# A hybrid decoder layer on eight cores: the mixer result added in DRAM, and other uses for the bf16 write-backs

## The reference

```
u1 = rmsnorm(x, ffn1_norm);   h = x + 0.5 * (silu(u1 @ Wg1) * (u1 @ Wu1)) @ Wd1
z = rmsnorm(h, mix_norm) @ w_in              # a_val a_gate | B C x | g_a g_b, 1024 columns each
a = causal_conv31(a_val * sigmoid(a_gate)) + bias;   a = silu(layernorm(a));   y_a = a @ a_w_out
y_b = (B * causal_conv3(C * x)) @ b_w_out
h = h + (sigmoid(g_a) * y_a + sigmoid(g_b) * y_b) @ w_o
h = h + 0.5 * (silu(u2 @ Wg2) * (u2 @ Wu2)) @ Wd2     # u2 = rmsnorm(h, ffn2_norm)
out = rmsnorm(h, final_norm)
```

## Time and profile before

| | |
|---|---|
| median of 3 runs | 3161.51 us (3161.02, 3161.51 and 3572.86) |
| the profiled execution | 3157.62 us |
| its span, slowest core (core 6) | 3156.1 us; the other cores 3136.4 to 3156.0 |
| PE / DVE / ACT / POOL busy | 96% / 78% / 28% / 6% |
| granted TensorE clock, mean | 0.988 of 2.4 GHz |
| DMA queue 1 (SP), queue 0 (POOL) | 42.6% and 28.8% of 16 engines |
| HBM | 231 GB/s read and written, mean over the span |
| the chain that ended last | PE 75%, DMA 19%, DVE 2%, issue 2% |

### The profile page before, as it was taken

The page is one execution under the profiler, slowest core; times in us unless marked ns, Lnnn a source line. Parts: engine busy times, 40 slices in busy tenths (PEclk is TensorE's granted clock), DMA queues, the critical chain, the costliest instruction groups (busy, mean ns, idle before and its releaser), DMA issues.

```text
span 3156.1 us, 45091 instructions; the slowest of 8 cores (3136.4 to 3156.1 us)
## 1 busy us (share of the span) xinstructions
PE 3036.5 (96%) x13885; PEld 1387.5 (44%) x14160; DVE 2461.9 (78%) x3458; ACT 876.5 (28%) x1572; POOL 197.0 (6%) x374
## 2 busy tenths in 40 slices
PE   7989999999999999979999999999999999999997
PEld 3434444444444444434444444444444444444445
DVE  2368999969996788858899889879898999896332
ACT  2222233223321224213241233232422332232221
POOL 1111001001110000000001000100000000000000
PEclk8999999999999999989999999999999999999998
DMA  9999959879999799995646555754656555645453
GB/s 185 185 220 195 251 162 193 211 206 209 167 212 256 229 226 234 226 263 189 221 151 196 185 175 176 213 177 149 216 157 221 186 165 187 202 161 186 146 187 123
DMA packets 183241, 615.26 MB, mean 195 GB/s; under 512 B 20896, under 2 KB 23072, under 8 KB 177248
## 3 DMA queue, kind: packets, MB, share of 16 engines
q1 hardware_dynamic: 134288, 432.11, 42.6%
q0 software_dynamic: 47200, 177.99, 28.8%
q10 hardware_dynamic: 1520, 2.27, 0.2%
HBM read 623.78 MB, written 103.81 MB: 231 GB/s over the span
## 4 chain that ended last, share of the span: by engine, by line
PE 75%; DMA 19%; DVE 2%; issue 2%; SPq 1%; ACT 0%; DVEq 0%; POOL 0%; ACTq 0%; POOLq 0%
PE ps L412 75%; DMA wbf<-wslot 9%; DMA wslot<-wpack 4%; DMA hst<-hs 3%; DVE acc L412 1%; DMA hs<-hst 1%; SPq L412 1%; DMA wslot<-wbf 1%; DMA hT<-xT 1%; DMA hs<-hT 0%; DVE hT L412 0%; DVE rstdX L412 0%; ACT sq L412 0%; DMA outT<-hT 0%; ACT L412 0%
## 5 line engine op out<-in xcount | busy, mean ns | idle before, releaser
L412 DVE SCALAR_TENSOR_TENSOR acc<-abuf,vecs_sb,acc 128x512 f32<-128x512 f32 x1920 | 1435.8, 749 | 132.7 <-ACT acc L412 8.9
L412 PE MATMUL ps<-uF,wslot 128*128 128x512 bf16 x5516 | 1246.9, 381 | 35.9 <-DMA wslot<-wpack 10.9
L412 PEld LDWEIGHTS ps<-uF,wslot 128*128 128x128 bf16 x5632 | 551.6, 98 | 708.1 <-issue 56.0
L412 PE MATMUL ps<-uM,wslot 128*128 128x512 bf16 x3517 | 793.4, 379 | 14.5 <-DVE acc L412 5.1
L412 PE MATMUL ps<-act,wslot 128*128 128x512 bf16 (+1 forms) x2938 | 628.6, 368 | 16.4 <-DMA wslot<-wpack 7.5
L412 ACT ACTIVATE fp<-ps 128x512 f32<-128x512 f32 x513 | 304.0, 595 | 1096.7 <-PE ps L412 1053.9
L412 PEld LDWEIGHTS ps<-uM,wslot 128*128 128x128 bf16 x3584 | 350.5, 98 | 436.9 <-issue 17.4
L412 PEld LDWEIGHTS ps<-act,wslot 128*128 128x128 bf16 x2992 | 293.7, 98 | 333.5 <-issue 20.9
L412 DVE TENSOR_TENSOR act<-fp,ps 128x512 bf16<-128x512 f32 x352 | 239.7, 682 | 216.9 <-PE ps L412 201.4
L412 ACT ACTIVATE sq<-hT 128x512 bf16<-128x512 f32 (+1 forms) x260 | 157.8, 612 | 599.2 <-DVE hT L412 570.9
L412 PE MATMUL ps<-acc,wslot 128*128 128x512 bf16 x1008 | 239.5, 381 | 3.8 <-DMA wslot<-wpack 2.9
(11 more groups left out here) (46 smaller groups left out, 934.5 us busy)
## 6 DMA issues: line engine op xcount, KB each, us to landing
wslot<-wbf SPq DMA_DIRECT2D x470, 512.0 KB, 4.6
wslot<-wpack POOLq DMA_DIRECT2D x170, 512.0 KB, 14.4
wslot<-wbf SPq DMA_DIRECT2D x203, 352.0 KB, 3.4
wbf<-wslot SPq DMA_DIRECT2D x80, 512.0 KB, 11.2
wslot<-wpack POOLq DMA_DIRECT2D x61, 352.0 KB, 11.9
hst<-hs POOLq DMA_DIRECT2D x59, 256.0 KB, 6.1
outT<-hT POOLq DMA_DIRECT2D x14, 1024.0 KB, 6.7
wslot<-wbf SPq DMA_DIRECT2D x48, 256.0 KB, 3.7
```

The costliest lines, as they stand in the source:

```text
L412: ins = getattr(E, meth)(*a, **kw)
```

## The change

1. **Add in DRAM.** In the output projection ScalarE copies half the matmul result to a buffer of the thg ring (four buffers, which the gates use too), and a DMA on POOL's queue adds it to hs in DRAM. The staged load, VectorE's add and the staged store go.
2. **Staging.** The four hst buffers all serve `normalize_staged`; four pieces are requested ahead, not two.
3. **Write-backs.** Of gu1 and dn1 slabs those with an index of 0 mod 6 stay at the first use, those of 1, 3 and 5 at the second, and those of 2 and 4 go to the third. All win, m3 and wo slabs are written at the third use; before, two of three were at the second. gu2 and dn2 stay at the second.
4. **First input.** Tile 1's input is requested no earlier than 50 us by the program's own clock.
5. **Last unit.** Four chunks are computed for all 512 positions, and four in halves, the second half in reverse. No slab is read again. The scale of the first half is spread over the second, and stores alternate between SP's and POOL's queues, not SP's and ACT's.

```diff
         if kk[0] in ("gu1", "dn1"):
-            return 0 if kk[1] % 6 == 0 else 1
+            return (0, 1, 2, 1, 2, 1)[kk[1] % 6]
         if kk[0] in ("gu2", "dn2"):
             return 1
-        return 2 if kk[1] % 3 == 1 else 1
+        return 2
...
-    def stage_store(self, t, k, r, i):
-        self.tr.dma(self.hq(), "sst%d" % i + self.hq(), self.b_hs[t][k], r, self.hs[t, :, k, :], self.stage[i][:], kb=256)
+    def stage_add(self, t, k, y, added):
+        self.tr.dma("pool", "sst%d" % (k % 4), self.b_hs[t][k], y, self.hs[t, :, k, :], y.ap, kb=512, accum=ALU.add)
+        added[0] += 1
+        if k == KC - 1:
+            self.m_out.add(t)
...
-    def stage_load(self, t, k, side):
-        i = 2 * side + self.st_i[side] % 2
-        self.st_i[side] += 1
...
         self.tr.dma(self.hq(), "sld%d" % i + self.hq(), b, self.b_hs[t][k], self.stage[i][:], self.hs[t, :, k, :], kb=256,
-                    slack=SLACK_S[side, self.b_pos <= CAST_POS])
+                    slack=SLACK_S[self.b_pos <= CAST_POS])
...
-        for k in range(2):
-            S[k] = self.stage_load(t, k, 0)
+        for k in range(NST):
+            S[k] = self.stage_load(t, k)
...
-            if k + 2 < KC:
-                S[k + 2] = self.stage_load(t, k + 2, 0)
+            if k + NST < KC:
+                S[k + NST] = self.stage_load(t, k + NST)
...
             if which == 2 and t not in self.m_out and t < NT - 1:
+                return
+            if q == 1 and tr.t["pe"] < X1_NS:
                 return
...
-        S = self.wo_stage
-        for i in range(2):
-            S[i] = self.stage_load(t, i, 1)
-
-        def put(i, hst, si):
-            self.stage_store(t, i, hst, si)
-            if i + 2 < KC:
-                self.defer(tr.ready([], [hst]), lambda: get(i + 2))
-            if i == KC - 1:
-                self.m_out.add(t)
-
-        def get(i):
-            S[i] = self.stage_load(t, i, 1)
+        added = [0]
         for i in range(KC):
-            yield ("wo", lambda: max(tr.ready(mm), tr.ready([S[i][0]])) if i in S else INF)
-            hst, si = S.pop(i)
+            yield ("wo", lambda: max(tr.ready(mm), self.w_ready(t, "wo", i // 2)) if added[0] >= i - 3 else INF)
             sbuf, st = self.slab(t, "wo", i // 2)
             ci = i % 2
             ps = self.bank()
             self.group(ps, [(st[:, (ci * 8 + k) * 128:(ci * 8 + k + 1) * 128], sbuf, mm[k]) for k in range(KC)])
-            tr.op("dve", lambda E: E.scalar_tensor_tensor(
-                out=hst.ap, in0=ps.ap, scalar=0.5, in1=hst.ap, op0=ALU.mult, op1=ALU.add),
-                reads=[ps, hst], writes=[hst], cost=690)
-            self.defer(tr.ready([hst]), lambda i=i, hst=hst, si=si: put(i, hst, si))
+            y = self.r_th.next()
+            tr.op("act", lambda E: E.activation(out=y.ap, in_=ps.ap, func=AF.Copy, scale=0.5),
+                  reads=[ps], writes=[y], cost=600)
+            self.defer(tr.ready([y]), lambda i=i, y=y: self.stage_add(t, i, y, added))
         self.c_done.add(t)
 
```

`X1_NS` is 50000.0. The accumulating DMA is `dma_start(..., accum_op=ALU.add)`. The core of the last unit:

```diff
-        for e in (0, 1):
-            nps = self.bank(hold=True)
-            for n, d in enumerate(range(KC) if e == 0 else reversed(range(KC))):
-                tk = t + (1 if e == 1 and n >= 4 else 0)
-                yield ("d", lambda: max(tr.ready(self.b_act), self.w_ready(tk, "dn2", 2 * d)))
...
+        nps = [self.bank(hold=True), self.bank(hold=True)]
+        seen = [0, 0]
+        steps = [((0, 1), d) for d in range(KC // 2)] + [((0,), d) for d in range(KC // 2, KC)] + \
+                [((1,), d) for d in reversed(range(KC // 2, KC))]
+        tail = []
+        for es, d in steps:
+            yield ("d", lambda: max(tr.ready(self.b_act), self.w_ready(t, "dn2", 2 * d)))
+            sb0, st0 = self.slab(t, "dn2", 2 * d)
+            sb1, st1 = self.slab(t, "dn2", 2 * d + 1)
+            lo, hi = es[0] * H, (es[-1] + 1) * H
...
+                tr.op("pe", lambda E, lap=lap, a=a, f=f: E.matmul(
+                    ps.ap[:, lo:hi], lhsT=lap, rhs=a.ap[:, lo:hi], start=(f == 0), stop=(f == FC - 1)),
+                    reads=[sbuf, a], writes=([ps] if f == 0 else []), mark=(f == FC - 1), cost=MM_NS * len(es) / 2)
...
+            if es == (1,):
+                if d == KC - 1:
                     self.flush(tr.ready([sq]) - 1.0)
-                    self.last_scale(t, 0, bh[0], rst[0], nps0)
-            if e == 0:
-                nps0 = nps
+                    assert seen[0] == KC
+                    tail = self.last_scale(t, 0, bh[0], rst[0], nps[0])
+                for _ in range(1 if d == KC - 1 else (2 if d > KC // 2 else 0)):
+                    tail.pop(0)()
         self.flush()
-        self.last_scale(t, 1, bh[1], rst[1], nps)
+        for fn in tail + self.last_scale(t, 1, bh[1], rst[1], nps[1]):
+            fn()
...
-                tr.dma("sp" if k % 4 == 1 else "act", "fin%d" % ((k // 2) % 2), self.b_out, x[k - 1],
+                tr.dma("sp" if k % 4 == 1 else "pool", "fin%d" % ((k // 2) % 2), self.b_out, x[k - 1],
```

More of the change, by code:

```diff
@@ L137 @@
 FEED_NS = 9000.0
+X1_NS = 50000.0
 INF = float("inf")
@@ L276, in op, with dma @@
         return tok
[L278 removed]
+    def dma(self, queue, semkey, out_buf, in_buf, out_ap, in_ap, extra_reads=(), extra_writes=(), kb=None, slack=0.0, accum=None):
         reads = _flat([in_buf] + list(extra_reads))
@@ L281, in dma @@
         self._waits(queue, reads, writes)
-        self.eng[queue].dma_start(out=out_ap, in_=in_ap).then_inc(self.sem[semkey], 16)
+        kw = {} if accum is None else {"accum_op": accum}
+        self.eng[queue].dma_start(out=out_ap, in_=in_ap, **kw).then_inc(self.sem[semkey], 16)
         self.cnt[semkey] += 16
@@ L388, in build @@
                        [k + q for k in ["xld%d" % i for i in range(NH)] + ["pst%d" % i for i in range(2 * NH)] +
-                        ["sld%d" % i for i in range(NST)] + ["sst%d" % i for i in range(NST)]
-                        for q in ("sp", "pool")] + ["misc", "fin0", "fin1"]
+                        ["sld%d" % i for i in range(NST)]
+                        for q in ("sp", "pool")] + ["sst%d" % i for i in range(4)] + ["misc", "fin0", "fin1"]
             sems = {k: st.enter_context(nc.semaphore(k)) for k in semnames}
@@ new lines, in last_down, with stat @@
+        nps = [self.bank(hold=True), self.bank(hold=True)]
[8 more added lines that the diff above has]
+            lo, hi = es[0] * H, (es[-1] + 1) * H
+            ps = self.bank()
+            for f in range(FC):
+                st, sbuf = (st0, sb0) if f < 11 else (st1, sb1)
+                lap, a = st[:, (f % 11) * 128:(f % 11 + 1) * 128], self.b_act[f]
+                tr.op("pe", lambda E, lap=lap, a=a, f=f: E.matmul(
+                    ps.ap[:, lo:hi], lhsT=lap, rhs=a.ap[:, lo:hi], start=(f == 0), stop=(f == FC - 1)),
+                    reads=[sbuf, a], writes=([ps] if f == 0 else []), mark=(f == FC - 1), cost=MM_NS * len(es) / 2)
+            ps.w = ("pe", tr.cnt["pe"])
+            ps.tw = tr.t["pe"] + 200.0
+            x = [bh[e][d] for e in es]
+            xap = self.hT[p][:, d, lo:hi]
+            tr.op("dve", lambda E: E.scalar_tensor_tensor(
+                out=xap, in0=ps.ap[:, lo:hi], scalar=0.5, in1=xap, op0=ALU.mult, op1=ALU.add),
+                reads=[ps] + x, writes=x, cost=225 + 225 * len(es))
+            sq = self.new_sq()
+            tr.op("act", lambda E: E.activation(out=sq.ap[:, lo:hi], in_=xap, func=AF.Square),
+                  reads=x, writes=[sq], cost=200 + 210 * len(es))
+            def stat(es=es, sq=sq):
+                for e in es:
+                    n = seen[e]
+                    seen[e] += 1
+                    b = nps[e]
+                    tr.op("pe", lambda E: E.matmul(b.ap[:, 0:H], lhsT=self.ones[:], rhs=sq.ap[:, e * H:(e + 1) * H],
+                                                   start=(n == 0), stop=(n == KC - 1)),
+                          reads=[self.b_ones, sq], writes=([b] if n == 0 else []), cost=MM_NS / 2)
+                    b.w = ("pe", tr.cnt["pe"])
+                    b.tw = tr.t["pe"] + 200.0
+            self.late.append((tr.ready([sq]), stat))
+            if es == (1,):
+                if d == KC - 1:
@@ L1002, in last_scale, with root, one @@
         H = T // 2
[L1003 to L1006, removed]
-        tr.op("dve", lambda E: E.reciprocal(out=rst.ap, in_=sd.ap[:, 0:H]), reads=[sd], writes=[rst], cost=1700)
-        V = self.vecs
-        for k in range(KC):
-            tr.op("dve", lambda E, k=k: E.scalar_tensor_tensor(
+        V = self.vecs
+        p = (2 * NT - 1) % NH
+        def root():
+            sd = self.r_f.next()
+            tr.op("act", lambda E: E.activation(out=sd.ap[:, 0:H], in_=nps.ap[:, 0:H], func=AF.Sqrt, bias=EPS, scale=1.0),
+                  reads=[nps], writes=[sd], cost=420, actset="sqrt")
+            self.release(nps)
+            tr.op("dve", lambda E: E.reciprocal(out=rst.ap, in_=sd.ap[:, 0:H]), reads=[sd], writes=[rst], cost=1700)
```

(6 more changed lines are left out.)

33 lines of the change are left out of this document (5 added, 28 removed).

## The result

The changed kernel takes 3210.08 us (median of 4 runs, the profiled one 3207.84), against 3163.12 for the kernel before (4 runs). The ratio is 1.0146, 95% interval 1.013 to 1.0162: slower by 47 us, clear of the noise, where 3158 was forecast in a range of 3130 to 3185. Medians over all runs contain a disturbed one (3572.86 before, 3600.94 after); the ratio does not, and the ranges given for the experiments leave such runs out.

What follows compares the result with a forecast made beforehand. The prediction saw TensorE 96% busy, with DMA nearly full until about 1440 us and half idle after. Its terms, -4 - 10 + 0 - 5 + 31 - 8 - 7.5, made -3.5, so 3158 us, range 3130 to 3185.

Steps and rivals of the forecast that it cites:

- Rival 4: Whole kernel: the planner lays out all work anew by changed costs, moving some holes, 10 us either way; no chance given.
- VectorE's in-order wait for hst<-hs: Output projection: the wait goes, gaining 10 us in 475 to 740, 5 in 940 to 1111, 8 in 2030 to 2080.
- Write-backs (-4 and +31): New write-back uses: 130 to 416 us gains 4; 1237 to 1440 loses 31 to 14 more casts with writes.
- 740 to 1111: Mixer projection of tile 2, merge and output of tile 1: 354 us of transfers fit in 371, cost 0.
- Rival 1: 1237 to 1540 us: the overload is absorbed into half-free DMA time, giving 3107 us, or 3094; chance 0.27.
- Rival 2: 1237 to 1440 us: casts wait 98 us for write-backs, 33 more; 3191 us, or 3221 with nothing absorbed earlier; chance 0.18.
- Rival 3: Four-buffer copy ring: copies wait for landed adds and ScalarE holds everything behind; 38 us, 3196; chance 0.08.
- The listed sign: Among the signs that would prove the forecast wrong: ScalarE shows waits on the adds; no size given.
- The add's price (1.6): Each 256 KB DRAM add takes 1.6 us of DMA, like a 256 KB cast; bounds 0.82 and 2.4.
- Last unit: End of kernel: dropping the down-weight reload gains 5.8 us of wait and about 1.7 at half clock, -7.5; final stores stay.
- First input (0): Delaying tile 1's input to 50 us starts work some 6 us earlier, but TensorE gives it back by 334: 0.

Runs made afterwards that it cites:

- e9: Kernel before with only the DRAM add and four-deep staging, order replanned; write-backs, first input and last unit of before: 3202.9 to 3210.4 us, 1.014.
- e13: Kernel before, exact order kept; VectorE writes half the matmul result and the store becomes a DRAM add on POOL's queue: 3161.4 to 3169.1 us, 0.9967.
- e11: e9 with the add planned 8 us longer (4 in the second half) and output groups waiting for their copy buffer: 3179.66 and 3181.22 us.
- e7: Kernel before with its order of work unchanged, only the transfers following the new write-back rule: 3196.9 to 3209.9 us, 1.0073.
- e8: Changed kernel with its order of work unchanged, only the transfers following the old write-back rule: 3197.2 to 3209.1 us, 1.008.
- e5: Changed kernel, TensorE and VectorE order kept; a tile's first four copies use idle buffers, each add its own semaphore: 3228.7 to 3231.8 us, 1.0171.
- e3: Changed kernel with the last unit of before (slabs read again, scale in one piece, stores on SP and ACT): 3196.6 to 3201.2 us, 1.0118.
- e6: Changed kernel with the last unit's eight output stores not waiting for one another: 3204.6 to 3226.2 us, 1.0119.
- e12: Kernel before with the last unit alone changed: no slab reread, first-half scale in one piece, unchained stores on SP and ACT: 3144.8 to 3159.5 us, 0.9969.
- e4: Changed kernel without the delay of tile 1's input: 3204.8 to 3229.4 us, 1.0164.
- e1: Changed kernel with the write-back rule of before: 3199.3 to 3199.9 us, 1.012.
- e2: Changed kernel without the DRAM add: staged residual added by VectorE and staging as before, all else of the change kept: 3302.5 to 3312 us, 1.0471.
- e15: e11 with the last unit of e12: 3181.5 to 3192.3 us, 1.0038.
- e14: e13 and e12 together, on the kernel before: 3150.3 to 3165.1 us, 0.9939.

## Why the prediction was wrong

Two steps failed. The larger is a term that the sum put at nothing: what the change does to the order laid out. Rival 4 ("The planner lays out all work anew by changed costs") bounded it at "10 us either way", with no chance and no place. The runs showed 55 us for it (e9 against e13). The smaller is the price of "**What goes for certain is VectorE's in-order wait for hst<-hs**", -10, -5 and -8: with the order held the add gained 10 us, not 23.

The trace of before speaks against the 23 as well. TensorE's waits in the whole span (engine and tile, what it waited for: us in total, times, longest), and the hole near 640:

```profile
PE ps L412 <- ACT sq L412: 33.2, 14, 6.3
...
PE ps L412 <- DVE hst L412: 7.2, 3, 5.6
...
653.71 1.15 ACT L412 ACTIVATE sq<-acc 128x512 bf16<-128x512 f32 x2 [7.71 <-DVE acc L412]
...
654.48 0.59 PE L412 MATMUL ps<-sq,ones 128*128 128x512 bf16 x1 [6.29 <-ACT sq L412]
```

Of the hole that got -10, 6.29 us end with a square that waited for VectorE's convolution results (acc), and 1.00 us with hst; VectorE itself had waited 4.24 us for the staged residual. In the whole span TensorE waits 7.2 us directly for hst. The forecast gave VectorE's wait the time that TensorE lost nearby.

- **The plan (forecast: 0, at most 10 us either way).** From the add in the old order to the add replanned it is 1.014/0.9967, 1.7% or 55 us. The new plan takes an output group as ready when its merge results and weights are, and no longer waits for a staged piece; e11 shows that pricing the add longer and waiting for its buffer brings back 26 us of it. The rest of the 55 us wasn't taken apart; it includes whatever the copy's engine and the staging depth do.
- **VectorE's wait (-10, -5, -8 forecast).** The wait at the output projection went, as told. With the order held nothing came in its place at the mixer's input (uM 27.7 us in e13, 32.9 before), and it was worth 10 us. In the new order uM's wait rose to 54.2 us (62.3 in e9), and fell to 23.5 in e11 with the same transfers: it is the order, too, that makes VectorE late there.
- **Write-backs (-4 and +31).** The mechanism is right: 1139 to 1461 lost 51.1 us at a share of 1.00, as asked for. With the order held the rule costs 23 us (e7) or 21 (e8), against +27. Rival 1, "absorbed", is out.
- **740 to 1111 ("It fits: 0", and -5 for the wait).** After loses 27.4 us from 717 to 1139, where before lost 7.6 from 740 to 1111. It isn't the casts: in the old order the same casts cost 12 loads there (e7, 1673 against 1685), in after's order with the old rule it is 1546 loads (e8).
- **Rival 2 (slot starvation, 3191 to 3221).** The measured 3210 lies between its values, and its signs are there: from 1139 to 1461 the casting queue waited 142.1 us for write-backs (64.3 before, 98 told). But the rule costs 21 to 23 us by itself, so the number would have been right by luck; and e13 has 301.8 us of that wait in all, more than before's 222.9, and is faster.
- **Rival 3.** ScalarE did wait for the adds, 110.1 us, just as told, and it cost nothing measurable (e5). The listed sign, "if ScalarE shows waits on the adds", was therefore a poor test: the waits were there, and they weren't the cost.
- **The add's price (1.6).** In after the packets of one add take 1.74 us of all 16 engines, so the term was 9% short. The Trainium skill ("Collectives: The Full Stack", "The bandwidth ceiling: the fold count and why AG ≠ RS ≠ AR") says of the reduce step of collectives that its add reads two sources for each write. The trace is in keeping with it, 1.74 against 0.77 us for a plain 256 KB, but shows no reads by themselves.
- **Last unit (-7.5, and "the stores behind the last matmul stay").** The reload's wait went, and the stores didn't stay: +11.6 us (24.4 against 12.8). e3 and e6 show it. The code had it in plain sight: one tracked output buffer, and first-half stores issued four steps later. Without the chain, and with the scale in one piece, the new last unit gains 10 us (e12).
- **First input (0).** e4 shows nothing against it.

Redone with what was measured one at a time, the sum is -10 (e13) + 22 (e7, e8) + 4 (last unit: 11.6 - 7.5) + 0 = +16; the other 34 of 50 us are put down to the order by subtraction. That the parts don't add up cleanly shows in e9 (the add and its plan alone cost 44 us, and the rule on top of it only some 8, by e1) and in e2. Left open: what makes the rest of the 55 us, and what keeps e15 a per cent behind e14.

## What to carry to other kernels

Where a program lays out a static order by its own costs, ask first what the edit does to the order: run the new operation once in the old order and once replanned, before anything is tuned. A wait that shows in the trace is a cost only if what is behind it would have been ready; take it out to know. And where transfers fill the time, a shorter dependency gains little, while a store spread "beside" other work must be followed to its queue and to the buffer it is tracked by.

## What the runs showed of the hardware

- An accumulating DMA from SBUF to DRAM of 256 KB takes 128 packets of 2048 bytes. From 1500 to 3080 us, where POOL's queue has no other packets of that size, their mean is 217.8 ns in after, 1.74 us of the 16 engines, and 204.6 to 211.7 ns in e9, e11 and e13, 1.64 to 1.69 us. The plain staged loads and stores of before take 64 packets of 4096 bytes there at a mean of 192.9 ns, 0.77 us. So an add costs 2.1 to 2.3 plain ones, 6 to 13% more than the load and the store that it replaces (1.54).
- Its issue occupies POOL longer than a plain one, a median 846 ns against 542. After's trace (instructions of POOL on the tile hs: count, duration ns min/median/max, first and last start):

```profile
L414 POOL DMA_DIRECT2D hs<-thg x56: 835/846/1562, 622.0 to 2647.8; - x56
...
L414 POOL DMA_DIRECT2D hs<-hT x6: 534/542/561, 1587.8 to 2497.1; - x6
```
